# The odd mixer's output product as three single-pass products of high and low halves, its rows spread through the last head pair

## The reference

```python
def odd_mixer(xn, w_in, w_o, cos_f, sin_f):
    b, s, _ = xn.shape
    hcat = (xn @ w_in).reshape(b, s, DIL_GROUPS, 3, DIL_HEADS, HEAD_DIM)
    q = apply_rope(hcat[:, :, :, 0], cos_f, sin_f)
    k = apply_rope(hcat[:, :, :, 1], cos_f, sin_f)
    v = hcat[:, :, :, 2]
    return dilated_attention(q, k, v) @ w_o
...
            x = x + odd_mixer(xn, od_w_in[o], od_w_o[o], cos_f, sin_f)
        x = x + sq_relu_mlp(rms_norm_2(x, norm_mlp[layer]), mlp_w1[layer], mlp_w2[layer])
```

## Time and profile before

| | |
|---|---|
| median of 3 runs | 1246.93 us (1245.67 to 1247.02) |
| the profiled execution: time, span | 1245.8 us, 1244.0 us |
| mean granted clock of TensorE in it | 0.995 |
| busy in the span: PE, PEld | 1182.6 us (95%), 1012.2 us (81%) |
| busy in the span: DVE, ACT | 734.9 us (59%), 549.3 us (44%) |

### The profile page before, as it was taken

How to read it: one execution, slowest core, us unless ns; L and a number is a source line. 1 busy time by engine, 2 the same in 40 slices (tenths; PEclk the granted TensorE clock), 3 DMA queues, 4 the chain that set the end, 5 groups by cost and what they waited for, 6 DMA issues and landing times.

```text
span 1244.0 us, 18713 instructions
## 1 busy us (share of the span) xinstructions
PE 1182.6 (95%) x7369; PEld 1012.2 (81%) x7369; DVE 734.9 (59%) x975; ACT 549.3 (44%) x727; POOL 52.0 (4%) x60
## 2 busy tenths in 40 slices
PE   4899998899999989899999999999999999999997
PEld 1577785689999978647999998999999975999996
DVE  1578336464555476755465465777777755654653
ACT  3862242343434352644243336655555534433432
POOL 2000033000000070000000000000000000000000
PEclk9999999999999989999999999999999999999999
DMA  9683471898655550707654535455555354655510
GB/s 316 212 286 128 137 271 43 297 255 265 189 174 169 164 129 1 255 17 257 212 170 175 182 102 148 126 133 152 152 152 152 86 195 160 236 171 206 173 58 35
DMA packets 201039, 209.72 MB, mean 169 GB/s; under 512 B 5803, under 2 KB 166838, under 8 KB 200790
## 3 DMA queue, kind: packets, MB, share of 16 engines
q1 hardware_dynamic: 197520, 201.61, 51.2%
q0 software_dynamic: 1648, 5.03, 1.6%
q10 hardware_dynamic: 1814, 2.30, 0.6%
HBM read 207.86 MB, written 2.01 MB: 169 GB/s over the span
## 4 chain that ended last, share of the span: by engine, by line
PE 83%; DVE 7%; DMA 3%; ACT 3%; SPq 2%; issue 2%; ACTq 0%; DVEq 0%
PE bank L1916 21%; PE bank L1918 20%; PE bank L1917 20%; PE bank L2170 2%; PE bank L1763 2%; PE bank L1765 2%; PE bank L1764 2%; DMA weight_pool<-in_mod_w_dram 2%; PE bank L2311 2%; SPq L454 2%; PE bank L2299 1%; PE bank L2289 1%; DVE work L1482 1%; PE bank L1714 1%; DMA normed<-in_ctx_dram 1%
## 5 line engine op out<-in xcount | busy, mean ns | idle before, releaser
L1916 PE MATMUL bank<-hT_high,mlp_up_high 128*128 128x256 f32 x512 | 145.2, 284 | 1.1 <-DVE hT_low L1384 1.1
L1917 PE MATMUL bank<-hT_low,mlp_up_high 128*128 128x256 f32 x512 | 144.9, 283 | 0.0
L1918 PE MATMUL bank<-hT_high,mlp_up_low 128*128 128x256 f32 x512 | 144.9, 283 | 0.0
L1916 PE MATMUL bank<-od_w_high,hT_high 128*128 128x384 f32 x384 | 132.7, 346 | 1.7 <-DVE hT_low L1384 1.4
L1918 PE MATMUL bank<-od_w_high,hT_low 128*128 128x384 f32 x384 | 128.7, 335 | 0.0
L1917 PE MATMUL bank<-od_w_low,hT_high 128*128 128x384 f32 x384 | 128.4, 334 | 0.0
L1073 DVE TENSOR_TENSOR mlp_down_low<-weight_pool,mlp_down_high 128x2048 fp32r<-128x2048 f32 x32 | 73.3, 2290 | 59.1 <-ACT mlp_down_high L631 59.1
L1916 PE MATMUL bank<-hT_high,ffn_up_high 128*128 128x256 f32 x352 | 99.7, 283 | 2.9 <-DVE hT_low L1073 2.9
L1916 PEld LDWEIGHTS bank<-hT_high,mlp_up_high 128*128 128x128 f32 x512 | 98.1, 192 | 2.9 <-issue 2.0
L1916 PE MATMUL bank<-mlp_down_high,hidden_high 128*128 128x512 f32 x256 | 99.9, 390 | 0.0
L1917 PE MATMUL bank<-mlp_down_low,hidden_high 128*128 128x512 f32 x256 | 99.9, 390 | 0.0
(11 more groups left out here) (324 smaller groups left out, 2629.3 us busy)
## 6 DMA issues: line engine op xcount, KB each, us to landing
weight_pool<-in_mlp_w_dram SPq DMA_DIRECT2D x64, 1024.0 KB, 7.6
weight_pool<-in_od_w_in_dram SPq DMA_DIRECT2D x72, 512.0 KB, 5.2
weight_pool<-in_mod_w_dram SPq DMA_DIRECT2D x22, 1024.0 KB, 10.5
weight_pool<-in_ffn_w_in_dram SPq DMA_DIRECT2D x44, 512.0 KB, 5.4
weight_pool<-in_gla_w_in_dram SPq DMA_DIRECT2D x12, 1024.0 KB, 6.2
weight_pool<-in_ffn_w_out_dram SPq DMA_DIRECT2D x22, 512.0 KB, 6.7
weight_pool<-in_gla_w_out_dram SPq DMA_DIRECT2D x2, 2048.0 KB, 14.5
weight_pool<-in_ev_w_in_dram SPq DMA_DIRECT2D x4, 1024.0 KB, 6.7
```

The costliest lines, as they stand in the source:

```text
L1916: mm(out_, left[0], right[0], start=start, stop=False, **flag)
L1917: mm(out_, left[0], right[1], start=False, stop=False, **flag)
L1918: return mm(out_, left[1], right[0], start=False, stop=stop, **flag)
```

## The change

The output product becomes three single-pass products like the others. The heads' outputs are kept as `heads_high` and `heads_low` (DVE now makes two passes over bank 7 in place of one copy), and each of the 8 rows of the weight gets a high half (`od_out_high(k)`, ACT) and a low half (`od_out_low(k)`, DVE, written over the loaded row). Halves of rows 0 to 2 are made during pair 7, those of rows 3 to 7 during `od_last`. The weights come in three loads (rows 0 and 1; 2 to 4; 5 to 7); the first is issued ahead of all projection weights, into a free place. The pieces on PE are put in another order. One wait is also changed everywhere in the odd mixer: `od_scores` waits for the maxima of the units before (`max_ready`), not for their exponentials (`prob_ready`). The diff shows, in this order, the places, SP's queue, ACT's stream (in its `od_pair`, m is None in the last pair), DVE's stream and PE's.

```diff
-        odT = view(work, 12800, KD, SEQ)
+        odT2 = [view(over(f"heads_{w}", "work", at, 2048), 0, KD, SEQ) for w, at in (("high", 12800), ("low", 18496))]
...
-        for i in range(2):
-            L["oo", i] = plan(f"od_out{i}", [0, 4096][i], [(0, (4, D), odo[:, 4 * i:4 * i + 4, :])], ("out_used", i + 5),
-                              ring=f"w_ring{i}")
+        for i, (k, n) in enumerate(((0, 2), (2, 3), (5, 3))):
+            L["oo", i] = plan(f"od_out{i}", OO_AT[k], [(0, (n, D), odo[:, k:k + n, :])], ("out_used", 6), ring=f"w_ring{i}")
+        plan("od_out_high", 6144, [(0, (2048,), None)], ("out_used", 6))
...
+            fetch(L["oo", 0])
             fetch_ring(L["od"], 3, lambda m, g: [odin[:, :, g, j, m, :] for j in range(3)])
-            fetch(L["oo", 0])
             fetch(L["oo", 1])
+            fetch(L["oo", 2])
...
                     od_values(m, pm, 0, 0)
+                if m is None:
+                    act.wait_ge(s["od_ps"], 6 * OD_PAIRS)
+                    od_out_high(3)
                 if n is not None:
                     od_turned(n, pn, 2)
+                if m is None:
+                    od_out_high(4)
...
+                if m is None:
+                    od_out_high(5)
                 if m is not None:
                     od_values(m, pm, 1, 0)
+                if isinstance(m, int) and m == OD_PAIRS - 1:
+                    od_out_high(1)
+                if m is None:
+                    turned_unit(u + 0, 0, 2 * n + PV0)
+                    turned_unit(u + 1, 1, 2 * n + PV0)
                 if n is not None:
                     exp_unit(u + 2, 2, 1, 1.0, od_col(pn, 2))
                     exp_unit(u + 3, 3, 1, 1.0, od_col(pn, 3))
+                if m is not None and n is not None:
                     turned_unit(u + 0, 0, 2 * n + PV0)
                     turned_unit(u + 1, 1, 2 * n + PV0)
...
+                if m is None:
+                    od_out_high(6)
...
             def od_out(n):
                 dve.wait_ge(s["pv_ps"], 2 * n + (PV0 + 2))
-                dve.tensor_copy(dilated(odT[:, n, :]), by_sma(bank[7][:, 0:SEQ])).then_inc(s["o_out"], 1)
+                hi, lo = (x[:, n, :] for x in odT2)
+                chain(dve.tensor_copy(dilated(hi), by_sma(bank[7][:, 0:SEQ])))
+                dve.tensor_tensor(dilated(lo), by_sma(bank[7][:, 0:SEQ]), dilated(hi.bitcast(F32)), ALU.subtract).then_inc(s["o_out"], 1)
+
+            def od_out_low(k):
+
+                e, at = oo_part(k)
+                dve.wait_ge(s["oo_hi"], OO_ORDER.index(k) + 1)
+                low(ooL[k][:, :], pool[:, e.at + at:e.at + at + D], ooH[k][:, :], "oo_lo")
...
-                pe.wait_ge(s["prob_ready"], u)
+                pe.wait_ge(s["max_ready"], u)
...
-                    e = L["oo", k // 4]
-                    if t == 0 and k % 4 == 0:
-                        landed_wait(e)
+                    pe.wait_ge(s["oo_lo"], OO_ORDER.index(k) + 1)
                     pe.wait_ge(s["o_out"], 8 + k + 1)
                     for b in (2 * t, 2 * t + 1):
-                        ins = mm(bank[b][:, :], odT[:, k, P * t:P * t + P], pv(e)[:, k % 4, 512 * (b % 2):512 * (b % 2) + 512],
-                                 start=(k == 0), stop=(k == KD - 1))
+                        ins = split_mm(bank[b][:, :], both(odT2, lambda x: x[:, k, P * t:P * t + P]),
+                                       both((ooH[k], ooL[k]), lambda x: x[:, 512 * (b % 2):512 * (b % 2) + 512]), k == 0, k == KD - 1)
...
                 od_scores(u + 2, pn, 1)
+                od_out(0, 4, 1)
                 od_turn_probs(u + 0, 0)
                 od_turn_probs(u + 1, 1)
-                od_out(0, 4, 2)
+                od_out(0, 5, 1)
                 od_attend(u + 0, pn, 0, n)
+                pe.wait_ge(s["qkT_out"], 3 * OD_PAIRS)
+                pe.wait_ge(s["max_ready"], U_OD + 4 * OD_PAIRS)
+                od_out(1, 0, 1)
                 od_turn_probs(u + 2, 2)
                 od_turn_probs(u + 3, 3)
-                od_out(0, 6, 1)
+                od_out(1, 1, 2)
                 od_attend(u + 2, pn, 1, n)
-                pe.wait_ge(s["qkT_out"], 3 * OD_PAIRS)
-                pe.wait_ge(s["pT_ready"], U_OD + 4 * OD_PAIRS)
-                od_out(1, 0, 4).then_inc(s["out_used"], 1)
-                od_out(0, 7, 1).then_inc(s["y_half"], 1)
-                od_out(1, 4, 4).then_inc(s["out_used"], 1)
+                od_out(1, 3, 3)
+                od_out(0, 6, 2).then_inc(s["y_half"], 1)
+                od_out(1, 6, 2).then_inc(s["out_used"], 2)
```

More of the change, by code:

```diff
@@ L256, in program @@
         raw = view(work, 6144, 2, 256)
-        odT = view(work, 12800, KD, SEQ)
+        odT2 = [view(over(f"heads_{w}", "work", at, 2048), 0, KD, SEQ) for w, at in (("high", 12800), ("low", 18496))]
+        OO_HIGH = [("normed", 0), ("normed", 1024), ("weight_pool", 6144)] + [("hT", 1024 * i) for i in range(4)] + [("weight_pool", 7168)]
+        ooH = [over(f"od_out{k}_high", where, at, D) for k, (where, at) in enumerate(OO_HIGH)]
+        OO_AT = (16384, 17408, 0, 1024, 2048, 3072, 4096, 5120)
+        ooL = [over(f"od_out{k}_low", "weight_pool", at, D) for k, at in enumerate(OO_AT)]
         frow = consts[:, C_OM:C_OM + D]
@@ L615, in raw_square @@
                 at = NS + 6 * n + t
-                act.activation(work[:, 20480:20480 + D], res[:, t, :], ACT.Square, accum_out=stat[:, at:at + 1]).then_inc(s["mean_ready"], 1)
+                junk = work[:, 15424:15424 + D] if n == 6 else work[:, 20480:20480 + D]
+                act.activation(junk, res[:, t, :], ACT.Square, accum_out=stat[:, at:at + 1]).then_inc(s["mean_ready"], 1)
                 act.wait_ge(s["mean_ready"], 2 * (n - 3) + t + 1)
@@ L1632, in od_pair @@
                     od_scale(u + 1, pn, 1)
+                if last_n:
+                    od_out_low(5)
+                if n is not None:
                     od_max(u + 2, 2)
```

56 lines of the change are left out of this document (41 added, 15 removed).

## The result

The changed kernel takes 1236.98 us (median of 6 runs, 1235.67 to 1241.53), the kernel before beside it 1246.3 (6 runs, 1243.63 to 1247.53): a ratio of 0.9923, 95% interval 0.991 to 0.9936.

What follows compares the result with a forecast made beforehand. PE was taken as the bound, 83% of the span on the last-ending chain. Savings of 2.0 us in the loop and 4.7 us in the last pair, 6.7 us together, gave a median of 1240.2 us, range 1238.0 to 1243.5.

Steps and rivals of the forecast that it cites:

- The loop wait: Loop pairs: PE's stop for ACT's exponential before the second scores goes, 0.34 us at 6 stops, 2.0 us saved.
- The product itself: Output product in the last pair: 64 x 0.432 us replaced by 96 x 0.228 us, 5.8 us less.
- Handing over: PE switching between fp32 and single-pass work: 1.6 us for 8 pieces, less 0.5 for old ones, takes back 1.1 us.
- Idle time: PE's last-pair waits, from a layout of the new order: 0.5 us of old idle goes, 0.15 us comes.
- DVE late at the updates: Residual updates after the output product: DVE starts late, 0.2 us lost, second transposes 4.7 us earlier.
- Loads and halves in pair 7: Weight loads and the halves made in pair 7: costed at nothing; 1.2 us lost if one half lay on the path.
- The small edits: Four small edits, costed at nothing because they add no instruction.
- A: Loop: the wait only changes owner, PE stops for DVE, the 2.0 us are lost; 1242.2 us, chance 0.17.
- B: Last pair becomes bound by DVE, PE waits before the first t = 1 piece; 1242 to 1243.5 us, chance 0.09.
- C: Last pair: high and low halves do not overlap at all, 4.7 us slower; 1251.6 us, chance 0.04.
- D: Nothing measurable: saved PE time only uncovers the wait for the MLP slabs; 1246.9 us, chance 0.03.
- E: Output product: single-pass products overlap better than in the MLP, 7.3 us more saved; 1232.9 us, chance 0.02.

Runs made afterwards that it cites:

- e1: The kernel before with only the wait of the second scores changed, to the maxima instead of the exponentials; 1244.32 us, ratio 0.9984.
- e8: Changed kernel with its last block cut into single rows, four fp32 transposes (work thrown away) in each of four gaps; 1239.59 us, one run.
- e3: Changed kernel with the pieces of the output product in the order of the kernel before, still three single-pass products; 1240.07 us, ratio 0.9954.
- e14: Changed kernel with four semaphores (final_loaded, zero_ready, place_ps, place_ready) made separate again; 1239.64 us in one run.
- e4: Changed kernel without the third of the three single-pass output products, all halves still made; 1235.36 us, ratio 0.991.
- e10: Changed kernel with last two rows bank by bank, earlier update of bank 2 and third MLP low half moved later; 1236.27 us, ratio 0.9908.
- e12: Changed kernel with its last block cut into single rows, four fp32 products on 64 array rows in each of four gaps; 1245.77 us, one run.
- e9: Changed kernel with its last block cut into single rows, four full 128 x 128 x 128 fp32 products in each of four gaps; 1243.03 us, one run.

## Why the prediction was right in direction and wrong in size

- **The loop wait** was forecast at 2.0 us and measured 2.05 in the changed kernel (262.51 to 260.46) and 2.10 alone (e1). DVE moves with PE, as argued; no wait took the place of the old one.
- **The product itself**: the pitch is as forecast. The last block's 42 records start between 1034.79 and 1044.21, 41 distances of 0.230 us.
- **Handing over is the step that failed.** The working said that a single-pass piece between two fp32 stages "costs 0.2 us extra, and there are 8 of them: 1.6 us". The 0.2 was read beside scores, which work on 64 rows of the array, and was put on every piece. Beside turns there is next to nothing of it (e8), and the cause is the array's shape, a change which the old product made at the same places as well. What the pieces take above 0.228 a record in the changed kernel adds up to about 1.2 us (0.07 to 0.24 each, the most between the two scores), and the stages of transposes between them are shorter than the layout had it: the turn 0.36 for 0.44, two turned units 0.79 (1030.06 to 1030.85) for 0.93, twice. In all some 0.8 us less than the 1.6: the term of 1.1 in the sum (1.6 less 0.5 for the old pieces) measured about 0.4. From first piece to the product's end it was 29.4 us (1015.00 to 1044.21 and one pitch), not 30.2.
- **Idle time**: the layout held. Two rows of product took 3.13 us up to the second scores, 0.2 more than the layout's 2.94; PE waited there for the maxima as forecast, 0.15 us (0.48 us from the last product's start to the scores, 1022.13 to 1022.61, against 0.33 at the first scores, 1018.08 to 1018.41; DVE's second maximum ended at 1022.56). At the layout's tightest place the fourth maximum ended at 1028.25 and PE came at 1028.57, 0.3 us of cover where the layout had 0.2. The order of the pieces was worth 1.8 us (e3).
- **DVE late at the updates**: the start of the last block to the first update took 8.7 us (1034.79 to 1043.47), forecast 8.9; the second transposes came 1.7 us behind the product, forecast 1.8. So the last pair gave 5.55 us, not 4.7: 0.85 more, of which the product's end is 0.76 and this the rest.
- **The heads' second pass**: 0.61 us was taken, 0.61 and 0.62 measured; hidden, as costed.
- **Loads and halves in pair 7**: at nothing, and right, since the first piece follows its projection with the same 0.39 us wait as before. The MLP's later slab cost nothing either: 182.41 us behind the second transposes against 182.42.
- **The small edits "at nothing"**: right for the semaphores (e14), but the end of the span is 0.45 us shorter with the change, which no term had.
- **The rivals**: A fell with e1, B in part (DVE does bound the last pair, but alongside PE, without a loss), C and D with the result, E by the pitch.
- **Slips in the working**: the products were said to end "some 33 us after the last projection where it was 36". Its own sum gives 31.3 (36.2 less 4.9), and 30.6 was measured (1013.84 to 1044.44).

From 1240.2 down to 1236.98 are 3.2 us: 0.85 for the last pair, 0.05 for the loop, 0.45 at the span's end, and 0.6 because before's own median was 1246.3 and not 1246.93. The other 1.3 us no trace accounts for. I take them for spread: all 17 runs of the changed kernel have a median of 1237.61, 0.6 higher, and they reach over 5.9 us. The range's second fault was there: its low end allowed 0.7 us for the spread of runs, taken from three. So that the time fell below the range is in part a low sample; that the last pair gave more than forecast is not.

## What to carry to other kernels

Price a handover from a stage with the same array shape on both sides (each row prints it, as 64\*128); between fp32 and single-pass work on the full array it was 0.04 us or less. When a product gets shorter in a stage shared with another engine, look for the next release that it will run into: here the wait edit and the shorter product were worth 0.9 us more together than apart, and what e4 took off PE beyond that was mostly lost to DVE. For effects under 1% measure a stretch between two fixed instructions in the trace, for here its length repeated to 0.05 us where whole runs differed by several.

## What the runs showed of the hardware

A change of TensorE's array shape and back costs 0.33 us (64 columns) or 0.40 us (64 rows) beyond full-array work; fp32 work between single-pass work costs 0.04 us or less. After PE had stood for 3.4 us in e4 its granted clock was 0.66 over the next 5 us, a mixture of its two levels (1.2 and 2.4 GHz), and 16 transposes took 3.7 us (1042.52 to the next instruction at 1046.20) where e10 needed 2.1; e4's first transposes came 1.9 us earlier after the mixer's start than the changed kernel's, the MLP's first product only 1.3. At a change of the array's shape the weight load no longer overlaps the product ahead of it: it started 0.33 us behind that product's start in e12, 0.01 in e9. The single-pass pitch at 512 columns was 0.228 to 0.230 us wherever it was read.
